# Differential attention placed between the q and g weight units, and v computed with x as the loaded operand

## The reference, cut to what matters

```python
k_sh = (x @ w_k_shared).reshape(B, T, 16, 128)
v_sh = (x @ w_v_shared).reshape(B, T, 8, 256)
qg = x @ w_qg                                  # 2048 x 4096
s = q @ k^T * 128 ** -0.5 - slope[h] * |tq - tk|    # 16 maps, masked by chunks of 64
p = softmax(s).reshape(B, 8, 2, ...)
attn = p[:, :, 0] - lam * p[:, :, 1]           # lam from exp of two dot products
o = attn @ v                                   # 8 heads of width 256
o = o * rsqrt(mean(o * o) + eps) * subln_g * (1 - lam_init)
x = layernorm(alpha * x + (o * silu(g)) @ w_out)
```

## Time and profile before

| | us |
|---|---|
| median of 3 runs | 2439.37 (2438.56 to 2440.69) |
| the profiled execution, its own time | 2442.36 |
| its span in the trace | 2440.2 |
| TensorE busy (matmuls) | 2290.0 |
| VectorE, ScalarE, GpSimd busy | 1507.5, 1099.3, 47.6 |
| mean granted TensorE clock | 0.975 of full speed |

### The profile page before, as it was taken

One profiled execution on the slowest core, in us unless ns is written; L12 is line 12 of the kernel. 1 busy time (PEld: TensorE's weight loads), 2 busy tenths in 40 slices (PEclk: granted clock), 3 DMA queues, 4 the chain that ended last, 5 costly groups with the idle time before them and its releaser, 6 DMA issues.

```text
span 2440.2 us, 41612 instructions
## 1 busy us (share of the span) xinstructions
PE 2290.0 (94%) x15838; PEld 1935.1 (79%) x15838; DVE 1507.5 (62%) x2070; ACT 1099.3 (45%) x1544; POOL 47.6 (2%) x51
## 2 busy tenths in 40 slices
PE   7997989999999999997999999999798999998796
PEld 6886768888888888886888778888386888887585
DVE  5555458885588757867856888422655544444754
ACT  5444455444444434445447554322334444445533
POOL 0003000000000000000000000000200000000100
PEclk9999999999999999998999999999798999999898
DMA  7663445666565666554645556200353566654052
GB/s 229 186 191 121 128 149 157 189 189 187 183 188 184 186 189 189 180 175 135 212 143 178 155 159 203 72 10 10 121 184 116 181 188 184 188 184 143 1 172 69
DMA packets 389255, 378.76 MB, mean 155 GB/s; under 512 B 33969, under 2 KB 387633, under 8 KB 388305
## 3 DMA queue, kind: packets, MB, share of 16 engines
q1 hardware_dynamic: 389138, 377.13, 50.2%
HBM read 370.79 MB, written 6.29 MB: 155 GB/s over the span
## 4 chain that ended last, share of the span: by engine, by line
PE 86%; DVE 9%; ACT 2%; issue 2%; DMA 0%; POOL 0%; SPq 0%; DVEq 0%; ACTq 0%; POOLq 0%
PE acc L644 48%; PE acc L645 24%; PE acc L913 3%; PE aux L913 3%; PE acc L668 1%; DVE w_lo L1600 1%; PE aux L727 1%; PE aux L865 1%; PE acc L669 1%; PE aux L831 1%; ACT w_hi L1096 1%; PE aux L851 0%; DVE inverse L2006 0%; DVE diff_scores L2182 0%; PE aux L999 0%
## 5 line engine op out<-in xcount | busy, mean ns | idle before, releaser
L1600 DVE TENSOR_TENSOR w_lo<-raw_w,w_hi 128x1024 fp32r<-128x1024 f32 (+1 forms) x592 | 706.8, 1209 | 580.8 <-ACT w_hi L1096 578.7
L1096 ACT ACTIVATE w_hi<-raw_w 128x1024 fp32r<-128x1024 f32 (+1 forms) x592 | 617.0, 1047 | 817.6 <-PE acc L645 798.1
L644 PE MATMUL acc<-h,w_hi 128*128 128x512 f32 x1856 | 653.5, 397 | 18.1 <-DVE w_lo L1600 16.9
L645 PE MATMUL acc<-h,w_lo 128*128 128x256 f32 x1856 | 520.3, 280 | 0.0
L644 PEld LDWEIGHTS acc<-h,w_hi 128*128 128x128 f32 x1856 | 349.4, 188 | 102.7 <-issue 17.6
L645 PEld LDWEIGHTS acc<-h,w_lo 128*128 128x128 f32 x1856 | 351.3, 189 | 0.0
L644 PE MATMUL acc<-x_split,w_hi 128*128 128x512 f32 x960 | 339.3, 399 | 1.7 <-DVE k_shared L1657 1.7
L645 PE MATMUL acc<-x_split,w_lo 128*128 128x256 f32 x960 | 269.6, 281 | 0.0
L644 PE MATMUL acc<-ff,w_hi 128*128 128x512 f32 x704 | 247.0, 395 | 2.4 <-DVE ff L1822 2.4
L644 PEld LDWEIGHTS acc<-x_split,w_hi 128*128 128x128 f32 x960 | 180.4, 188 | 46.9 <-DVE k_shared L1657 2.0
L645 PE MATMUL acc<-ff,w_lo 128*128 128x256 f32 x704 | 197.2, 280 | 0.0
(11 more groups left out here) (311 smaller groups left out, 3074.1 us busy)
## 6 DMA issues: line engine op xcount, KB each, us to landing
raw_w<-in_w_up SPq DMA_DIRECT2D x176, 512.0 KB, 3.4
raw_w<-in_a_w_in SPq DMA_DIRECT2D x128, 512.0 KB, 3.7
raw_w<-in_w_in SPq DMA_DIRECT2D x64, 512.0 KB, 3.6
raw_w<-in_w_down SPq DMA_DIRECT2D x64, 512.0 KB, 3.5
raw_w<-in_b_w_qg SPq DMA_DIRECT2D x64, 512.0 KB, 3.6
raw_w<-in_w_o SPq DMA_DIRECT2D x32, 512.0 KB, 3.5
raw_w<-in_a_w_out SPq DMA_DIRECT2D x32, 512.0 KB, 3.5
raw_w<-in_w_k_shared SPq DMA_DIRECT2D x32, 512.0 KB, 3.5
```

The source lines that it names most:

```text
L644: pe.matmul(out, wh, op[:, kt, :, :].rearrange("p h t -> p (h t)"), start=first, stop=False)
L645: mm = pe.matmul(out[:, 0:T], wl, op[:, kt, 0, :], start=False, stop=last)
L1096: act.activation(WHI[:, u % 4, 0:ku, :], RAWW[:, u, 0:ku, :], ACT.Copy).then_inc(hi_made, 1)
L1600: dve.tensor_tensor(WLO[:, u, 0:ku, :], RAWW[:, u, 0:ku, :], WHI[:, u % 4, 0:ku, :].bitcast(F32), ALU.subtract)\
```

## The change

**v.** The roles of the operands are swapped: 128 tokens of x are loaded, and 512 weight columns stream by (w_hi of two units at once, w_lo, and w_hi again for x's low part). The sum over the three products is made in the bank, the output lies with tokens on partitions, and ScalarE copies the bank straight to `v_shared_tok`. The transposes, `v_shared` and its join go. The v units are loaded in depth order, and TensorE frees two at a time.

**The attention** is cut into its steps, and these are put behind units n = 0 to 63 of the q and g products: `scores` of head h, one map each, behind units 8+4h and 10+4h, `turn` behind 15+4h, `pv` behind 18+4h. ScalarE and VectorE have their own lists, by the index of the unit whose split they have just done: distances at 11+4h and 13+4h with the maxima, exponentials at 14+4h, probabilities at 15+4h, copy of the turned ones at 18+4h, the head's output at 21+4h. The scores use one auxiliary bank for both maps, so each waits for the read of the last. The squares of four heads are summed at once, in four groups of 32 partitions (behind units 34 and 50), and the widening is a matmul of 32 rows per head, at `WIDE_AT`. Gating moves from GpSimd to VectorE (`GATE_AT`) and behind the scaling. Silu of g runs pair by pair.

**The output projection** begins with `first_body`, gated on pairs of `o_split` tiles; `by_depth` is set for its loads and evacuations. For the split of its first eight units the lists run on to n = 71.

The diff, cut to its core:

```diff
-            KS5, VS5, Q5, G5 = (sb(s1, n, [P, KD, T]) for n in ("k_shared", "v_shared", "q_diff", "silu_g_diff"))
+            KS5 = sb(s1, "k_shared", [P, KD, T])
+            VT5 = sb(s1, "v_shared_tok", [P, 2, KD, P])
+            Q5, G5 = (sb(s1, n, [P, KD, T]) for n in ("q_diff", "silu_g_diff"))
...
-            OSQ = sb(s1, "o_squares", [P, 2, 2, T])
-            EXP5 = sb(s1, "row_expand", [32, D // 2])
-            RS5 = sb(s1, "o_rstd_rows", [32, 2, T])
+            OSQ = sb(s1, "o_squares", [P, 4, 2, T])
+            RS5 = sb(s1, "o_rstd_rows", [P, 2, T])
...
+        def diff_steps(n, first, per=4, over=8):
+
+            return [h_ for h_ in range(over) if first + per * h_ == n]
+        WIDE_AT = [38, 41, 44, 47, 55, 57, 59, 61]
+        GATE_AT = [42, 46, 50, 54, 59, 61, 65, 68]
+        BEFORE_Q = ALL_TILES + 2 * KD + 8
...
+                if not iters:
+                    return
...
-            sp.dma_start(EXP5[:, :], h["consts"][0:32, CCOL["expand"]:CCOL["expand"] + D // 2]).then_inc(dist_in, 16)
-            for n, w in enumerate((h["w_k_shared_2"], h["w_v_shared_2"])):
-                weights(4, lambda i, b: (w, i * 512 + b * 256), by_depth=512 * (n == 0))
+            weights(4, lambda i, b: (h["w_k_shared_2"], i * 512 + b * 256), by_depth=512)
+            for i in range(4):
+                weights(1, lambda i_, b: (h["w_v_shared_2"], i * 512 + b * 256), by_depth=512)
             weights(8, lambda i, b: (h["b_w_qg_2"][0], i * 512 + b * 256))
-            weights(4, lambda i, b: (h["b_w_out_2"][0], i * 512 + b * 256))
+            weights(4, lambda i, b: (h["b_w_out_2"][0], i * 512 + b * 256), by_depth=512)
...
-            for n in range(8):
-                pool.wait_ge(o_out, n + 1)
-                pool.tensor_tensor(Q5[:, 2 * n:2 * n + 2, :], Q5[:, 2 * n:2 * n + 2, :], G5[:, 2 * n:2 * n + 2, :], ALU.mult).then_inc(o_gated, 1)
...
-                body()
+                (first or body)()
```

TensorE:

```diff
             first_body(A5, pairs_of(operand))
-            for n in range(4):
-                gemm(4 - (n == 0), A5, [])
-            pe.wait_ge(acc_free, seen.total(acc_free) + 4)
-            pe.wait_ge(lam_prod, 1)
-            pe.matmul(AUX[0][:, 0:2], ONES, LAM[:, 0:2], start=True, stop=True).then_inc(lam_sum, 1)
-            for n in range(8):
-                if n >= 4:
-                    pe.wait_ge(v5_tok, n - 3)
-                for j in range(4):
-                    mm = pe.transpose(ACC[n % 4][:, j * P:(j + 1) * P], VS5[:, 4 * (n % 4) + j, (n // 4) * P:(n // 4 + 1) * P], IDENT)
-                mm.then_inc(v5_turned, 1)
...
+            gemm(3, A5, [])
+
+
+            for i in range(4):
+                for q in range(4):
+                    pe.wait_ge(lo_made, seen(lo_made, 2))
+                    if q == 0:
+                        pe.wait_ge(acc_free, seen(acc_free, 2))
+                    wh, wl = WHI[:, 2 * q % 4:2 * q % 4 + 2, :, :], WLO[:, 2 * q:2 * q + 2, :, :]
+                    for k in range(4):
+                        kt = 4 * q + k
+                        for t_ in range(2):
+                            out = ACC[2 * (i % 2) + t_]
+                            xh, xl = (A5[:, kt, x, t_ * P:(t_ + 1) * P] for x in range(2))
+                            pe.matmul(out, xh, wh[:, :, k, :], start=(kt == 0), stop=False)
+                            pe.matmul(out, xh, wl[:, :, k, :], start=False, stop=False)
+                            mm = pe.matmul(out, xl, wh[:, :, k, :], start=False, stop=(kt == KD - 1))
+                    mm.then_inc(unit_done, 2)
+
+
+            def scores(n, m):
+                if m == 0:
+                    pe.wait_ge(acc_free, 4 + BEFORE_Q + 2 * n + 2)
+                if n + m:
+                    pe.wait_ge(d_read, 2 * n + m)
+                for q in range(2):
+                    mm = pe.matmul(AUX[0][:, q * T:(q + 1) * T], Q5[:, 2 * n + m, q * P:(q + 1) * P],
+                                   KS5[:, 2 * n + m, :], start=(q == 0), stop=(q == 1))
                 mm.then_inc(d_scored, 1)
...
-                if n >= 2:
-                    pe.wait_ge(o_out, n - 1)
-                out = ACC[n % 2]
+                if n >= 1:
+                    pe.wait_ge(o_out, n)
+                else:
+                    pe.wait_ge(acc_free, 4 + BEFORE_Q)
                 for d in range(2):
-                    pe.matmul(out[:, d * T:(d + 1) * T], VT5[:, 0, 2 * n + d, :], PT5[:, n % 2, 0:T], start=(d == 0), stop=False)
-                    mm = pe.matmul(out[:, d * T + P:(d + 1) * T], VT5[:, 1, 2 * n + d, :], PT5[:, n % 2, T:384], start=False, stop=(d == 1))
+                    pe.matmul(AUX[3][:, d * T:(d + 1) * T], VT5[:, 0, 2 * n + d, :], PT5[:, n % 2, 0:T], start=(d == 0), stop=False)
+                    mm = pe.matmul(AUX[3][:, d * T + P:(d + 1) * T], VT5[:, 1, 2 * n + d, :], PT5[:, n % 2, T:384], start=False, stop=(d == 1))
                 mm.then_inc(d_pv, 1)
...
+            def o_sums(r):
+
+                pe.wait_ge(o_out, 4 * r + 4)
+                if r:
+                    pe.wait_ge(o_scaled, 4)
+                for d in range(2):
+                    for c in range(4):
+                        mm = pe.matmul(AUX[1][32 * c:32 * c + 32, 0:T], PAIRSEL[:, 30:62], OSQ[:, c, d, :], start=(d == 0), stop=(d == 1))
+                mm.then_inc(o_sum, 1)
+
+            def o_widen(n):
+                r, at = n // 4, 32 * (n % 4)
+                pe.wait_ge(o_rstd, r + 1)
+                if n % 4:
+                    pe.wait_ge(o_scaled, n)
+                pe.matmul(AUX[1][:, T:], IDENT[at:at + 32, at:at + 1].broadcast_to([32, P]), RS5[at:at + 32, r, :], start=True, stop=True)\
+                    .then_inc(o_wide, 1)
+
+            for n in range(64):
+                pe.wait_ge(lo_made, seen(lo_made))
+                unit(A5, n // 4 % 2, n % 4, n % 8)
+                if n == 0:
+                    pe.wait_ge(lam_prod, 1)
+                    pe.matmul(AUX[0][:, 0:2], ONES, LAM[:, 0:2], start=True, stop=True).then_inc(lam_sum, 1)
+                if n == 7:
+                    pe.wait_ge(lam_exp, 1)
+                    pe.wait_ge(dist_in, 16)
+                for h_ in diff_steps(n, 8):
+                    scores(h_, 0)
+                for h_ in diff_steps(n, 10):
+                    scores(h_, 1)
+                for h_ in diff_steps(n, 15):
+                    turn(h_)
+                for h_ in diff_steps(n, 18):
+                    pv(h_)
+                if n in (34, 50):
+                    o_sums((n - 34) // 16)
+                if n in WIDE_AT:
+                    o_widen(WIDE_AT.index(n))
+            gemm(4, C5, [], side=sum_of(X, AUX[1]), first=lambda: first_body(C5, [(o_ready, 2 * n + 2) for n in range(8)]))
```

ScalarE:

```diff
-            pend = gemm(4, copier(), pending=pend, keep=True)
-            pend = gemm(4, copier(HEAD_SCALE), pending=pend, keep=True)
-            pend = gemm(4, silu_out(G5), pending=pend, keep=True)
-            split(0, between=pend)
-            act.wait_ge(lam_sum, 1)
-            act.activation(LAM[:, 2:4], AUX[0][:, 0:2], ACT.Exp).then_inc(lam_exp, 1)
-            for n in range(8):
-                act.wait_ge(v5_turned, n + 1)
-                act.activation(VT5[:, n // 4, 4 * (n % 4):4 * (n % 4) + 4, :], ACC[n % 4][:, :].rearrange("p (a b) -> p a b", a=4), ACT.Copy)\
-                   .then_inc(v5_tok, 1)
...
+            def v_out(i):
+                act.wait_ge(unit_done, seen(unit_done, 8, "tile"))
+                seen(acc_free, 2, "tile")
+                for t_ in range(2):
+                    act.activation(VT5[:, t_, 4 * i:4 * i + 4, :], ACC[2 * (i % 2) + t_].rearrange("p (a b) -> p a b", a=4), ACT.Copy)\
+                       .then_inc(acc_free, 1)
+
+            for i in range(4):
+                split(0, between=(lambda: v_out(i - 1)) if i else pend)
+                split(1)
...
+            def head_out(n):
+                act.wait_ge(d_pv, n + 1)
+                if n >= 4:
+                    act.wait_ge(o_sum, 1)
...
+            def head_hi(n):
+                act.wait_ge(d_scored, 16)
+                act.wait_ge(d_pv, 8 if n >= 4 else 1)
+                act.wait_ge(o_gated, n + 1)
                 act.activation(C5H[:, 2 * n:2 * n + 2, :], Q5[:, 2 * n:2 * n + 2, :], ACT.Copy).then_inc(o_hi, 1)
...
+            def pair_out(p_):
+                act.wait_ge(unit_done, seen(unit_done, 4, "tile"))
+                seen(acc_free, 2, "tile")
+                low_out(p_ % 2 * 2, HEAD_SCALE if p_ < 8 else 1.0)
+
+            def diff_silu(n):
+                act.wait_ge(acc_free, seen(acc_free, 0, "tile"))
+                d = G5[:, 2 * n:2 * n + 2, :]
+                act.activation(d, d, ACT.Silu).then_inc(g_ready, 1)
+
+            for n in range(64 + 8):
+                if n == 3:
+                    v_out(3)
+                elif n % 4 == 3 and n < 68:
+                    pair_out(n // 4 - 1)
+                if n == 67:
+                    diff_silu(7)
```

(124 more changed lines are left out.)

116 lines of the change are left out of this document (32 added, 84 removed).

## The result

The changed kernel takes 2396.26 us (median of 4 runs, 2393.04 to 2403.17), the kernel before 2438.97 (4 runs, 2435.41 to 2440.69): ratio 0.9831, 95% interval 0.9805 to 0.9856. Measured again in two later sets of rounds it gave 2396.12 (6 runs; ratio 0.9822, 0.9795 to 0.9848) and 2398.26 (5 runs; ratio 0.9823, 0.9804 to 0.9842). The forecast was 2396, faster.

A forecast was written before the change was run, and what follows sets the result against it. TensorE, busy 94% of the span, was taken as the bound, with time to gain only where it idles or runs slowly. -77.4 + 35.5 - 2.3 + 2.8 - 2.2 = -43.6 from 2442.4 gives 2398.8; median 3.0 lower: 2396, range 2386 to 2411.

The forecast's parts named there:

- (a): Differential attention alone, after the q and g units: the stretch disappears as a stretch, -77.4 us.
- (b): Attention's TensorE work returns as blocks between the 64 q and g units, +35.5 us; only part-array blocks pay a switch.
- Rival one: Blocks between q and g units: full-size ones pay the array switch too, +8.5 us, 2404; chance 0.10.
- (c): Start of the output projection: the slow-clock start goes because TensorE no longer waits, -2.3 us.
- (d): Output projection's first eight units in depth order: TensorE stands behind them, +2.6, and at the entry, +0.2; together +2.8 us.
- cold start: Output projection's first 4.6 us at clock 0.51, doing 2.3 us of work, after attention; expected to go, -2.3 us.
- The entry: Start of the output projection: banks 2 and 3 wanted 1.41 us after the last g unit, freed in about 1.5; +0.2.
- (e): v's new form: 384 matmuls of 512 columns at 0.23 us, 88.3 us against 90.5 before, -2.2.
- Rival three: v at the fast bound and pairs at the projection's pace: 5.4 and up to 5 us less, 2386 to 2391; chance 0.09.
- (f): VectorE and ScalarE attention work, table loads and queue order hidden beside the units: cost nothing, 5.9 us of slack left.
- Rival two: Slack of the in-order queues used up in places: one to three us per head, 2404 to 2420; chance 0.12.
- rival four: Each head's 6.2 us chain stands on TensorE's path, ScalarE's pv wait holding back w_hi: 49.6 more, 2446; chance 0.03.

The follow-up runs named there:

- read_first_o: Changed kernel, VectorE reading the first two finished banks before its split of the third unit, not the fourth, in the output projection only; 2394.88 us, ratio 0.9821.
- v_alone: Kernel before with only v in its new form, attention still behind all units, no v transposes; 2438.54 us, ratio 0.9999.
- pv_three_later: Changed kernel with pv of head h put behind unit 21+4h instead of 18+4h; 2456.86 us (one run).
- pv_two_later: Changed kernel with pv of head h put behind unit 20+4h instead of 18+4h; 2421.36 us (one run).
- read_first_all: Changed kernel with finished banks read before the third unit's split, on ScalarE and VectorE, in all four products that begin in depth order; 2395.19 us, ratio 0.9825.

## Why the prediction was right, step by step

The total was 2396.3 for 2396 forecast, which is closer than the steps were and in part luck, since their errors cancelled: +2.3 in the projection and +0.4 behind it, against -1.2 in v and -1.1 ahead of k, where nothing was changed. The changed kernel's own median also moves between sets of rounds (2396.1 to 2398.3).

(a) The stretch: -77.5 for -77.4. Nothing of it came back as a wait: no row for `d_probs`, `d_pt` or `o_out` on TensorE's side.

(b) The work put back: +35.50 for +35.5, by the stretches. By single blocks (excess over a pair's 0.353): one map's scores 0.862 (forecast 1.73 for two), turn 0.327 (0.33), pv 1.31 (1.30), sums 1.20 (1.2), widening 0.82 (0.77), lambda's sum 0.22 (not priced). They make 36.1; pairs that ran in part at the faster pace give the rest back. Rival one (full-size blocks pay the switch) is out: at the edges of the full-size blocks no start lies later than the passes explain. A map's scores in the changed kernel, between two units:

```profile
2134.51 0.28 PE L650 MATMUL acc<-x_split,w_lo 128*128 128x256 f32 x1
2134.63 1.03 PE L1049 MATMUL aux<-k_shared,q_diff 128*128 128x256 f32 x4
2135.30 0.58 PE L649 MATMUL acc<-x_split,w_hi 128*128 128x512 f32 x1
2135.72 0.28 PE L650 MATMUL acc<-x_split,w_lo 128*128 128x256 f32 x1
```

From 2134.51 to the second short matmul, 2135.72, it is 1.21; a pair takes 0.35, so the block costs 0.86, four passes of 0.216 and nothing for coming and going.

(c) and (d), the step that failed: "+2.8" for the depth order and "-2.3" for the cold start, together +0.5; measured +2.8. The gap was sized well: 2.70 from the start of the last pass to that of the next, less one step, for 2.6. The entry cost the 0.2 of the last wait shown above (0.2 forecast). What the prediction left out is that a gap of that length is followed by 3.4 us at 1.2 GHz, +1.7; it had taken the cold start away and did not ask whether its own new gap would bring one. The rows spoke for not asking: the 1.84 us gap behind k's first units is followed by no drop of the clock (1.00 from 1899.80 on). read_first_o takes both away and shows 4.3 us for them. Of the +2.3, the gap's size is 0.1 and the clock 1.7; what is left, about 0.5, is of the size that the pace moves.

(e) v: 87.07 us for 88.3. The matmuls start 0.2267 apart, as these rows of the changed kernel show over three steps:

```profile
2034.34 0.39 PE L1037 MATMUL acc<-w_hi,x_split 128*128 128x512 f32 x1
2034.57 0.39 PE L1038 MATMUL acc<-w_lo,x_split 128*128 128x512 f32 x1
2034.80 0.39 PE L1039 MATMUL acc<-w_hi,x_split 128*128 128x512 f32 x1
2035.02 0.39 PE L1037 MATMUL acc<-w_hi,x_split 128*128 128x512 f32 x1
```

0.68 for three; 384 times 0.2267 is 87.1. The price of 0.23 was read from one pair of starts rounded to 0.01. The same 87.05 to 87.10 came in all eleven executions that have this form, so this form showed one pace where the pairs showed two. The Trainium skill, "TensorE: Matmul & The Clock Gate", Back-to-back issue gap, gives 216 ns; the estimate of 82.9 us for v from it lies 4.2 us below the trace. Rival three needed v at that fast bound, and is out. That the new v form gains nothing in the total when it stands alone was not in the prediction. Its own 3.4 us are there in v_alone too; part of what it gives is lost in the thin attention stretch behind it, where the clock falls. The woven kernel has no such stretch.

(f) What was laid at nothing cost nothing. The prediction had unit 22+4h ready 6.0 us after the block behind unit 18+4h begins and wanted at 11.9. In the changed kernel that block begins at 2126.53:

```profile
2128.90 0.84 ACT L1606 ACTIVATE q_diff<-aux,params 128x256 f32<-128x256 f32 x2 [3.87 <-PE aux L1069]
2129.63 0.60 ACT L1607 ACTIVATE o_squares<-aux 128x512 f32<-128x512 f32 x1
2130.11 1.06 ACT L1127 ACTIVATE w_hi<-raw_w 128x1024 fp32r<-128x1024 f32 x1
```

```profile
2131.20 1.23 DVE L1667 TENSOR_TENSOR w_lo<-raw_w,w_hi 128x1024 fp32r<-128x1024 f32 x1 [1.47 <-ACT w_hi L1127]
```

w_lo ends at 2132.43, 5.9 us after the block's start, and TensorE takes unit 22+4h at 2138.32, 11.8 after: 5.9 us of slack. Three units' more delay of pv (8.5 us and the blocks between) exceeds that, and pv_three_later showed the 3.6 us per head that it must then cost. Two units' delay (5.7 us and a block) comes to about the slack, and already cost 21.7 us. So the slack as worked out is real for one hand-over, but the loop through scores and distances is nearer its end than this one list shows: in pv_two_later TensorE waited 8.2 us for the distances' read of the scores bank, against 7.2 for w_lo. Five more table loads were expected; the trace has 20 for 15, and seven lie in the q and g stretch, where TensorE has no gap. Rival two did not happen, rival four only where it was forced.

## What to carry to other kernels

Work that one engine can't fill by itself belongs between units of work that never wait; price the blocks by distances between starts, and the in-order queues by the slack from each wait to when its followers are wanted, and then test that slack by moving one step. Ask of each gap left or made whether the clock falls behind it: here a 2.7 us gap cost 4.3, and one of 2.56 elsewhere cost no clock. Ask of each reordering in a queue what it makes late: one of these moved the wait instead of removing it. Where unchanged code has two paces, judge a change of 3 us by its own stretch of the trace, not by the total.

## What had not been expected of the hardware

The pair of fp32r matmuls runs at 346.7 or 353.3 ns in the same code at the same clock, from execution to execution, while the 512-column form stays at 226.7. Taking away work at the head of a thinly used stretch left the total where it was, and 32 unused transposes made it faster, with the granted clock of the first 20 us at 1.00 for 0.76. And the length of a gap alone does not tell whether the clock falls behind it. The gap of 2.5 us behind the projection's first eight units (by the idle time in the timelines) was followed by half clock in all six executions that have it, the one of 1.7 us behind k's by full clock in all that have it. But in read_first_all a gap of 1.86 us, ahead of 1046.13, was followed by half clock, and the one of 2.56 us ahead of 1161.20 by full clock:

```profile
1047.30:1050.70 3.40, 3.40 (x13) 2.92 (x12) 1.78 (x3) 1.03 (x2) 0.00 (x0) 0.50 0.01 4
...
1161.20:1164.60 3.40, 3.40 (x19) 2.97 (x20) 3.40 (x4) 0.21 (x1) 0.00 (x0) 1.00 0.18 62
```

And of the gaps of 3.62 us in pv_three_later the one ahead of 2157.76 was followed by full clock, the one ahead of 2177.77 by half:

```profile
2157.76:2162.00 4.24, 3.05 (x16) 2.42 (x16) 2.46 (x4) 4.24 (x9) 0.00 (x0) 1.00 0.00 0
...
2177.77:2184.00 6.23, 6.23 (x21) 5.36 (x21) 4.34 (x10) 4.34 (x9) 0.00 (x0) 0.56 0.00 0
```

What decides it was not tried.
